# A two-layer hybrid token mixer: a third of layer 0's modulation up front, the rest as half products inside projection groups

## The reference, cut to what matters

```python
for i in range(DEPTH):
    sh1, sc1, g1, sh2, sc2, g2 = split(silu(c) @ mod_w[i] + mod_b[i], 6)       # latent
    ch1, cs1, cg1, ch2, cs2, cg2 = split(silu(c_ctx) @ mod_w[i] + mod_b[i], 6)  # context
    hl = rms_norm(x, norm_mix[i]) * (1.0 + sc1) + sh1
    hc = rms_norm(xc, norm_mix[i]) * (1.0 + cs1) + ch1
    yc, yl = mixer(hc, hl, ...)
    x = x + g1 * yl
    x = x + g2 * swiglu(rms_norm(x, norm_ffn[i]) * (1.0 + sc2) + sh2, ...)
    # the same for xc with ch2, cs2, cg1, cg2, where there is a next layer
```

## Time and profile before

| | |
|---|---|
| median of 3 runs | 2557.9 us (2553.79 to 2558.45) |
| the profiled execution's own time | 2555.26 us |
| its span, first to last instruction | 2553.4 us |
| busy share of the span: PE, DVE, ACT | 86%, 35%, 20% |
| chain that ended last: PE, DVE, DMA | 71%, 20%, 3% |
| mean granted TensorE clock | 0.915 of full |
| moved by DMA, mean rate | 193.38 MB, 76 GB/s |

### The profile page before, as it was taken

The page is one execution under the profiler, slowest core; times in us unless marked ns, Lnnn a source line. Parts: engine busy times, 40 slices in busy tenths (PEclk is TensorE's granted clock), DMA queues, the critical chain, the costliest instruction groups (busy, mean ns, idle before and its releaser), DMA issues.

```text
span 2553.4 us, 27229 instructions
## 1 busy us (share of the span) xinstructions
PE 2195.9 (86%) x11254; PEld 1357.4 (53%) x11254; DVE 882.8 (35%) x1797; ACT 498.6 (20%) x1013; POOL 130.3 (5%) x134
## 2 busy tenths in 40 slices
PE   4799866999788779999999999999736777799997
PEld 0347744478455544344444436445425455587886
DVE  0153266200899950100000015553157546401001
ACT  1211111241111210200000013111513344601000
POOL 0000121000000000000000000000012422100000
PEclk9699878999988989999999998999857888899999
DMA  9411100111333102122222212222000000033442
GB/s 356 165 54 66 50 1 0 59 59 66 116 132 123 42 17 74 66 72 77 82 69 76 74 66 88 77 74 91 33 1 2 2 2 21 31 116 132 148 151 97
DMA packets 27704, 193.38 MB, mean 76 GB/s; under 512 B 2972, under 2 KB 4125, under 8 KB 5566
## 3 DMA queue, kind: packets, MB, share of 16 engines
q1 hardware_dynamic: 27538, 191.51, 21.1%
q10 hardware_dynamic: 44, 0.14, 0.0%
HBM read 190.59 MB, written 1.05 MB: 75 GB/s over the span
## 4 chain that ended last, share of the span: by engine, by line
PE 71%; DVE 20%; ACT 4%; DMA 3%; issue 2%; SPq 0%; POOL 0%; ACTq 0%; DVEq 0%; POOLq 0%
PE psum L563 70%; DVE ws_sb L1453 7%; DMA ring_sb<-w 3%; DVE ws_sb L1640 2%; DVE ring_sb L1453 2%; DVE gl_tmp_sb L1453 2%; DVE wide_sb L1453 2%; DVE arena_sb L1453 1%; ACT ws_sb L1107 1%; DVE hT_sb L1456 1%; ACT L1107 1%; ACT wide_sb L1107 1%; DVE ws_sb L1456 0%; ACT arena_sb L1107 0%; PE psum L705 0%
## 5 line engine op out<-in xcount | busy, mean ns | idle before, releaser
L563 PE MATMUL psum<-hT_sb,ring_sb 128*128 128x512 f32 (+1 forms) x2256 | 806.0, 520 | 21.0 <-ACT hT_sb L1107 16.7
L563 PEld LDWEIGHTS psum<-hT_sb,ring_sb 128*128 128x128 f32 x2256 | 431.6, 192 | 386.7 <-issue 354.1
L563 PE MATMUL psum<-arena_sb,ring_sb 128*128 128x512 f32 (+1 forms) x1216 | 397.0, 488 | 3.6 <-DVE small_sb L1459 1.9
L1107 ACT ACTIVATE ws_sb<-psum 128x512 f32<-128x512 f32 (+3 forms) x208 | 133.4, 641 | 971.3 <-PE psum L563 893.6
L563 PEld LDWEIGHTS psum<-arena_sb,ring_sb 128*128 128x128 f32 x1216 | 232.5, 191 | 166.2 <-issue 144.5
L563 PE MATMUL psum<-ring_sb,hT_sb 128*128 128x256 f32 (+4 forms) x1312 | 252.3, 381 | 11.2 <-ACT hT_sb L1107 11.2
L563 PE MATMUL psum<-ws_sb 64*64 64x128 f32 (+3 forms) x1200 | 181.7, 314 | 79.9 <-DVE ws_sb L1453 46.8
L563 PEld LDWEIGHTS psum<-ring_sb,hT_sb 128*128 128x128 f32 (+1 forms) x1312 | 209.9, 190 | 54.9 <-issue 17.6
L563 PEld LDWEIGHTS psum<-ws_sb 128*128 128x128 f32 (+1 forms) x1200 | 152.9, 200 | 124.5 <-DVE ws_sb L1453 61.9
L1453 DVE TENSOR_TENSOR arena_sb<-ws_sb,psum 128x512 f32<-128x512 f32 (+1 forms) x44 | 24.4, 554 | 418.3 <-PE psum L563 418.3
L563 PE MATMUL psum<-const_sb,arena_sb 64*128 64x256 f32 (+3 forms) x576 | 128.9, 438 | 43.3 <-DVE ws_sb L1453 27.2
(11 more groups left out here) (127 smaller groups left out, 1508.0 us busy)
## 6 DMA issues: line engine op xcount, KB each, us to landing
ring_sb<-w SPq DMA_DIRECT2D x170, 1024.0 KB, 4.9
ring_sb<-w SPq DMA_DIRECT2D x8, 768.0 KB, 4.2
const_sb<-consts SPq DMA_DIRECT2D x1, 2496.0 KB
xT_sb<-x SPq DMA_DIRECT2D x1, 2048.0 KB
y<-xT_sb SPq DMA_DIRECT2D x1, 1024.0 KB, 4.8
ring_sb<-w SPq DMA_DIRECT2D x2, 256.0 KB, 2.8
const_sb<-consts SPq DMA_DIRECT2D x1, 512.0 KB, 5.6
cols_sb<-cols SPq DMA_DIRECT2D x1, 197.5 KB
```

The lines of the kernel that those rows point to most:

```text
L563: return nc.tensor.matmul(o, l, r, start=start, stop=stop)
L1107: return nc.scalar.activation(o, i, func, **kw)
```

## The change

- Of the 12 pieces of layer 0's modulation only the first four (`MOD_FIRST`) are computed up front: 8 blocks and not 24. They hold `sh1` and `sc1`.
- The other 8 pieces are 16 half products. Each is issued by PE between the tile f = 0 and the tile f = 1 of a projection group: in `xbc` after groups' first tiles 0 to 5, in all four groups of `z0` and `qk0`, and in groups 0 and 1 of `r0` (`LATE_AT`). Their blocks stand in the plan behind the block of their group, so that they alternate in the ring. They accumulate in PSUM bank 4. A finished row is copied by ACT to `late_row` (`late_copy`), turned into columns by PE ahead of the next piece's first half (`late_columns`, 8 MATMUL rows, bank 5), and taken by DVE (`late_taken`).
- In the part up front, PE does two `norm_sum` after each piece and turns the piece before into columns, where it had done all columns and then all sums at the end. ACT's squares and copies are interleaved in the same way. DVE adds the bias for 16 and not 48 columns, and forms the gain of the mixer only; the gain of the SwiGLU block is formed before the GLA scan.
- On the SP queue the six small constant matrices and `pick` are loaded first (448 KB in two transfers), after columns and rows. `xT` goes behind the second weight block, with a semaphore of its own. The other 32 constant matrices (2048 KB) go ahead of the first block of `z0`; PE waits for them at the GLA scan, and DVE too.
- Waits that guard banks 4 and 5, `late_row` and the later uses of the modulation stand ahead of `ssd`, of `v0` and of `gla`; the wait for `gk` moves from `gla` to ahead of `r0`. The memset of PSUM on DVE covers five banks and not four.

```diff
+MOD_FIRST = 4
+LATE = 12 - MOD_FIRST
+LATE_AT = {"xbc": (0, 6), "z0": (6, 4), "qk0": (10, 4), "r0": (14, 2)}
...
+    def with_late(name, n):
+
+        groups = []
+        at, n_late = LATE_AT[name]
+        for g in range(n):
+            p.stage(name, [([(CB, KC)], 2)])
+            groups += p.stages[name]
+            if g < n_late:
+                p.late.append(p.block("late", 2 * CB, KC // 2, None if (at + g) % 2 else 0))
+        p.stages[name] = groups
...
-            sp.dma_start(const[:, :, :], consts[:, 0:NCONST, :]).then_inc(s_in, 16)
             sp.dma_start(cols[:, :], cols_in).then_inc(s_in, 16)
             sp.dma_start(rows[:, :], rows_in).then_inc(s_in, 16)
-            sp.dma_start(xT[:, :, :], x_in.rearrange("p (a b) -> p a b", b=T)).then_inc(s_in, 16)
+            sp.dma_start(const[:, 0:6, :], consts[:, 0:6, :]).then_inc(s_in, 16)
+            sp.dma_start(const[:, NCONST - 1:NCONST, :], consts[:, NCONST - 1:NCONST, :]).then_inc(s_in, 16)
...
+                if n == 2:
+                    sp.dma_start(xT[:, :, :], x_in.rearrange("p (a b) -> p a b", b=T)).then_inc(s_x, 16)
+                if n == plan.stages["z0"][0][0][0]:
+                    sp.dma_start(const[:, 6:NCONST - 1, :], consts[:, 6:NCONST - 1, :]).then_inc(s_levels, 16)
...
+            def late_half(n):
+
+                if n % 2 == 0 and n > 0:
+                    late_columns(n // 2 - 1)
+                block = plan.late[n]
+                w = slot(block, 2 * CB, KC // 2)
+                block_ready(block)
+                for c in range(KC // 2):
+                    last = mm(psum[32 * c:32 * c + 2, 4, :], csilu[:, n % 2 * KC // 2 + c, :], w[:, c, :],
+                              start=(n % 2 == 0), stop=(n % 2 == 1))
+                last.then_inc(s_used if n % 2 == 0 else S["late_rows"], 1)
+
+            def late_columns(q):
+
+                pe.wait_ge(S["late_copied"], q + 1)
+                if q > 0:
+                    pe.wait_ge(S["late_taken"], q)
+                for t in range(4):
+                    last = mm(psum[:, 5, 2 * t:2 * t + 2], late_row[:, t * P:(t + 1) * P], cm("pick")[:, 0:2])
+                last.then_inc(S["late_columns"], 1)
...
             def modulation0():
                 pe.wait_ge(S["banks_zeroed"], 1)
-                for q in range(12):
+
+                def columns(q):
+                    drained(pe, out_of("mod0", q))
+                    for t in range(4 * q, 4 * q + 4):
+                        last = mm(psum[:, 4, 2 * t:2 * t + 2], mod_row[:, t * P:(t + 1) * P], cm("pick")[:, 0:2])
+                    return last
+
+                for q in range(MOD_FIRST):
                     ids, b = plan.stages["mod0"][q]
                     bank_free(b)
                     mod_products(ids, b % 4).then_inc(s_done, 1)
...
+                    norm_sum("mix0", 2 * q)
+                    norm_sum("mix0", 2 * q + 1)
+                    if q > 0:
+                        columns(q - 1)
+                columns(MOD_FIRST - 1).then_inc(S["mod_columns"], 1)
```

More of the change, by code:

```diff
@@ L199, in wide, with mod_half, mod, with_late @@
                 r += kc
-    def mod(i):
-        for j in range(12):
+    def mod_half(i, j, half):
+        put(w["mod_w"][i], half * D // 2, KC // 2, j * 2 * CB, 2 * CB)
+    def mod(i, n):
+        for j in range(n):
             for half in range(2):
-                put(w["mod_w"][i], half * D // 2, KC // 2, j * 2 * CB, 2 * CB)
+                mod_half(i, j, half)
+    def with_late(name, mat, c0, n):
+        at, n_late = LATE_AT[name]
+        for g in range(n):
+            wide(mat, c0 + g * CB, 1)
+            if g < n_late:
+                mod_half(0, MOD_FIRST + (at + g) // 2, (at + g) % 2)
     def tail(i, w_out):
@@ L599, in gemm @@
                             last.then_inc(s_done, 1)
+                        if f == 0:
+                            between(stage, g)
                     if i < len(ids) - 1:
@@ L1107, in f, with mod_copy, late_copy @@
                 return nc.scalar.activation(o, i, func, **kw)
[L1109 to L1114, removed]
+            def mod_copy(q):
+                b = out_of("mod0", q)
+                act.wait_ge(s_done, b + 1)
+                f(mod_row[:, q * 512:(q + 1) * 512], psum[:, b % 4, :], ACT.Copy).then_inc(s_drained[b % 4], 1)
+                act.wait_ge(s_drained[b % 4], b // 4 + 1)
+            def late_copy(q):
+                act.wait_ge(S["late_rows"], q + 1)
+                if q > 0:
+                    act.wait_ge(S["late_columns"], q)
+                own(f(late_row, psum[:, 4, :], ACT.Copy).then_inc(S["late_copied"], 1), S["late_copied"])
             def norm(tag):
@@ L1170, in conv_stage @@
                         activate(t - 1)
+                    if stage == "xbc" and t % 4 == 3:
+                        late_copy(t // 4)
                 activate(n_tiles - 1)
@@ L1217, in gla @@
                         for i in range(2):
+                            if stage == "r0" and (g, i) == (1, 1):
+                                late_copy(7)
                             b = out_of(stage, g, i)
@@ L1534, in conv_stage @@
                         evac(t - 2)
+                    if stage == "xbc" and t in (6, 10):
+                        late_taken(t // 4 - 1)
                 evac(info["tiles"] - 2)
@@ L1595, in gla @@
             def gla():
+                for q in (4, 5):
+                    late_taken(q)
                 for j in range(TT):
```

89 lines of the change are left out of this document (61 added, 28 removed).

## The result

The changed kernel takes 2500.56 us (median of 4 runs, 2499.12 to 2501.61) where the kernel before took 2555.85 us on the same chip. The medians differ by 55.3 us. The ratio estimated from the single executions is 0.977, with a 95% interval from 0.9746 to 0.9793, which is 53 to 65 us less. Forecast were 2503 us and a saving of 53.6. The profiled execution has a span of 2499.5 us, 53.9 under that of before. In two more comparisons the changed kernel came to 0.9762 and 0.9766 of the kernel before.

What follows compares the result with a forecast made beforehand. Bound: DMA loading up front while PE waits, PE in the projections. 75.8 us gained in front minus 22.2 inserted is 53.6 less; 2555.3 becomes 2501.7, plus 2.6 for the median 2504.3, stated as 2503; range 2494 to 2524.

Steps and rivals of the forecast that it cites:

- The front: Part before the first projection: start at 45.3 us, middle of 41.4 to 49.2, not 121.10; 75.8 us gained.
- The branch in which DMA is the bound: Front with PE at full clock: block 7 used at 31.9 us, norm sums done at 35.5, projections at 41.4.
- the branch in which PE is the bound: Front with PE at half clock, 8.7 us a piece: last norm sums done at 43.3 us, projections at 49.2.
- rival 1: Front at full clock: products 0.92, norm sums 0.86, projections at 40.4 us, total 2499; chance 0.14.
- The inserted work: Late pieces in the projections: 16 halves at 0.915 and 8 column sets at 0.95, 22.2 us, all on PE's path.
- Rival 2: Insertions pull the clock down in the projections: only 3 to 18 us less, 2540 to 2555; chance 0.08.
- The cover of the blocks: Inserted half's block in the projections: lands in 4.9 us, needed after 6.9, leaving 2.0 us, so no wait.
- rival 3: Each inserted half waits for its block mid-group; a landing of 11 us would give 2570; chance 0.03.
- the byte count of the prediction: Front landings from bytes queued ahead, 2.44 us a block: block 0 at 7.3 us, `xT` at 14.6.
- The rest: SSD, the GLA scan and everything after: shifted by about 54 us and otherwise unchanged.

Runs made afterwards that it cites:

- e9: The changed kernel with e8's order of inputs, sums and copies, front blocks kept in the ring of three slots: 2496.68 us, 0.976 of the kernel before.
- e10: The changed kernel run again without an edit, beside e11 on one chip: 2500.62 us, 0.9766 of the kernel before.
- e1: The changed kernel with the eight even half products each issued three times, same output: 0.9831 of the kernel before.
- e2: The changed kernel with all inserted halves but the first ahead of their group's first tile, not between tiles: 2582.88 us, 1.0087 of the kernel before.
- e5: The changed kernel with all twelve pieces up front and none inserted, new input order and interleaving kept: 2527.43 us, 0.9876 of the kernel before.
- e4: The changed kernel with the front's norm sums and columns after all four pieces, not interleaved: 2503.61 us, 0.9782 of the kernel before.
- e3: The changed kernel with all constants in one transfer ahead of everything and `xT` ahead of the weights: 2504.16 us, 0.9777 of the kernel before.
- e8: The changed kernel with front blocks in their own region, `xT` ahead of weights, norm sums and ACT's copies reordered: 2493.91 us, 0.9755 of the kernel before.
- e11: The kernel of e8 run again, beside e10 on one chip: 2492.66 us, 0.9735 of the kernel before.

## Why the prediction was right

**The front.** 75.8 us were forecast, 76.9 measured, with the start at 44.22 against 45.3. DMA and PE are the bound in turn, as the chain below shows, so a start between the two branches of the forecast was to be expected; that it came out within 1.1 us of their exact middle is luck. The middle is no mechanism, and the same kernel started its projections between 41.6 and 46.0. The branch in which DMA is the bound had block 7 used at 31.9, and it was used at 35.38; the branch in which PE is the bound had the projections at 49.2, 5 us too late. These two errors cancel. Two terms inside were off. `xT` was put at 14.6 by counting bytes, and its squares began at 17.08; block 0 was put at 7.3 and used at 9.77. The chain of waits shows the transfer of `xT` from its issue at 3.37:

```profile
3.37 13.63 DMA xT_sb<-x
...
28.26 7.07 DMA ring_sb<-w
```

Bytes ahead of a transfer gave its landing 2.4 us too early. In e9, where `xT` stands right behind the small constants, it is the same: 4.88 us of transfer less give 9.8, and it landed at 12.13. Why is not shown. Block 7 is out by 3.5 us: its transfer began at 28.26, when PE had freed the slot, and took 7.07. From the other side, the work after it was quicker: I had a piece at 8.7 us, and the trace has the second norm sums at 24.46, the third at 29.40, 4.9 us apart, since PE had come to the full clock. That was rival 1. Of its price, 0.92 a half and 0.86 a norm sum, pieces 2 and 3 (counted from 0) came near, while piece 0 ran at 1.89 and 1.75 a half and 3.78 for two norm sums, about as before. The page "TensorE: Matmul & The Clock Gate" of the Trainium skill, Part 1, has a busier PE run faster; in the later part of the front the trace agrees, with column rows at 0.95 for eight, and against the earlier trace rows, where PE was just as busy at half the clock, it does not. In e10 the clock fell again in piece 2, behind a wait of 2.25 us (a half at 1.88, norm sums 3.78 for four rows), and the start was 46.0; the wait of 2.24 us ahead of block 7 in the first profile did not bring that. So the front runs at either level in one and the same kernel, and no run here shows what decides it.

**The inserted work.** 22.2 us were forecast and 23.5 measured in the stages, but the term was 3.0 too small: by the pitches the insertions cost 25.2, and `small0` gave back 1.6 by its clock. The 0.915 taken from the GLA scan is the mean of two halves in a row; a first half has a pitch of 0.97 and one behind it 0.86 (e1). 16 x 0.97 + 8 x 0.88 = 22.6 are the rows themselves. The other 2.6 us are the 0.1 by which a dense tile right beside a half takes longer, which the forecast had at nothing. That all of it is on PE's path was right. Rival 2, the falling clock, did not happen between the tiles, and e1 shows that it doesn't with three halves in a row either.

**The cover of the blocks.** 2.0 us of cover were forecast, landing at 4.9 and need at 6.9. In `xbc` of the changed kernel the median landing was 5.5 over inserted and group blocks alike, so the cover was thinner but held, and there was no wait. e2 shows what happens without it, which is rival 3's wait. Its longest waits, 5.1 us with nothing between release and use, are the landing of an inserted block itself. The twelve waits add up to 50 us, and 26 more come that I hadn't priced, since a wait of 4 us for a block costs clock as well as time. Two thirds of e2's 81 us would have been enough to eat up the whole gain.

**What comes by which part.** The prediction had counted the front as one sum. e5 parts it: with all pieces up front 31.7 us come from the order of inputs, sums and columns, and then about 27 from the late pieces. e4 parts it the other way: with the late pieces there, the interleaving adds 3 to 5 us. e3 puts the order of the inputs at 1.9 us of start; this is less than the byte count of the prediction would say (4.9), since the landing of `xT`, and not only that of the last block, decides when PE begins. The total of e3 leaves open whether that is 1.9 or some 5 us.

**The rest.** What stands behind the GLA scan kept its length within 1.4 us together, as forecast. The GLA scan was forecast unchanged and is 2.7 us shorter. So the saving of 53.9 in the profiles is met to 0.3 by errors that cancel: 1.1 more in front, 1.3 more paid in the stages with insertions, 0.5 won elsewhere.

## What to carry to other kernels

Where a stage is bound by loading and another by PE, move loading and not work: the late pieces cost PE about 25 us of work that it had done beside transfers before, and paid because 16 blocks at 2.97 us had been waited for. A block that takes a slot freed only at the end of the group before it must not be needed at once; the distance from that release to its use has to be longer than a landing, and a wait that breaks a dense stream costs its length and then the half clock behind it, here half as much again. When the last transfer of a phase has landed, only what depends on it should be left to do; sums that need another input belong ahead of it, and ACT's in-order program has to be written with the same care as PE's.

## What the runs showed that was not expected

The SSD scan has the same work in all kernels, and took 163.6 to 164.5 us in six profiles and 166.1 to 167.2 in eight (its granted clock is 0.82 in e4 and 0.81 in the changed kernel). Both lengths occur with one and the same kernel: e8 has 167.2, and e11, which is e8 again, 164.2. It is why e4's late start was partly given back in its profile, and why a single profile's end can't price a few us in front of it. What decides between them stays open.

`small0` has the same work in all kernels too, and took 17.4 us in nine profiles, among them all of the changed kernel, and 19.0 to 21.0 in the five others. So the 1.6 us that it gave back was not owed to less work.

The GLA scan took 300.0 to 300.1 us in the kernel before and in e5, and 297.4 to 298.6 in all twelve profiles with late pieces. In its first 32 us the granted clock is 0.95 in the kernel before and 1.00 in the changed one. That stretch alone does not decide the length: in e1 it has 0.89, and the scan took 298.0 us. Over the whole scan the length goes with the clock: 0.90 before (300.0 us), 0.91 in e3 (298.6), 0.93 in e1 (298.0) and in the changed kernel (297.4). Whether the inserted work ahead of the scan has to do with that was not tried.
